# Early half products of the first up and input weight tiles, placed in the tails of the two projections before them

## The reference, cut to what matters

```python
y_l = merge_groups(conv_l, attn_l, w_o, b_o)              # cat @ w_o + b_o
x_mid = layer_norm(ALPHA * x + g1 * y_l, ln1_g, ln1_b)
h = x_mid * (1 + sc2) + sh2
u = dwconv(h @ w_up, dw_w, dw_b)                          # 1024 -> 2 * 2816
g, val = jnp.split(u, 2, axis=-1)
f_l = (silu(g) * val) @ w_down + b_down                   # 2816 -> 1024
x = layer_norm(ALPHA * x_mid + g2 * f_l, ln2_g, ln2_b)
# second block: rms_norm, scale and shift, then the second input projection
z = h2 @ w_in_2
```

## Time and profile before

| | us |
|---|---|
| median of 3 runs | 2505.81 |
| lowest and highest | 2502.83, 2510.84 |
| profiled execution, whole | 2498.72 |
| its span | 2496.8 |
| busy in the span: PE, PEld, DVE, ACT, POOL | 2275.4, 1130.6, 862.4, 485.3, 385.9 |

### The profile page before, as it was taken

How to read it: one execution, slowest core, us unless ns; L and a number is a source line. 1 busy time by engine, 2 the same in 40 slices (tenths; PEclk the granted TensorE clock), 3 DMA queues, 4 the chain that set the end, 5 groups by cost and what they waited for, 6 DMA issues and landing times. The chain is left out here.

```text
span 2496.8 us, 25488 instructions
## 1 busy us (share of the span) xinstructions
PE 2275.4 (91%) x9835; PEld 1130.6 (45%) x9835; DVE 862.4 (35%) x1468; ACT 485.3 (19%) x937; POOL 385.9 (15%) x755
## 2 busy tenths in 40 slices
PE   6998988999998998999967999888879999999985
PEld 3443654443443443444334488535434444444432
DVE  3456843222221130001888533423711111111116
ACT  2013552111110011001235422101011111111111
POOL 0004000400000000000000000000044444444424
PEclk9999999999999998998868999998989999999997
DMA  8502002455424113981202100302089999899867
GB/s 365 208 37 82 29 1 90 154 196 181 146 86 156 47 68 127 382 312 47 76 9 91 63 3 3 135 34 84 1 352 394 413 383 375 335 415 376 360 254 284
DMA packets 68553, 446.42 MB, mean 179 GB/s; under 512 B 12227, under 2 KB 12883, under 8 KB 43505
## 3 DMA queue, kind: packets, MB, share of 16 engines
q0 software_dynamic: 36176, 254.42, 25.8%
q1 hardware_dynamic: 32290, 190.78, 19.8%
HBM read 416.27 MB, written 73.45 MB: 196 GB/s over the span
## 5 line engine op out<-in xcount | busy, mean ns | idle before, releaser
L2533 PE MATMUL psum<-arena 128*64 128x512 f32 (+1 forms) x1088 | 360.6, 595 | 0.8 <-DMA arena<-in_exp_gu,arena 0.8
L938 PE MATMUL psum<-arena 128*128 128x512 f32 x704 | 307.2, 596 | 3.3 <-PEq L870 3.3
L2533 PEld LDWEIGHTS psum<-arena 128*64 128x64 f32 (+1 forms) x1088 | 138.8, 164 | 186.1 <-issue 185.1
L938 PEld LDWEIGHTS psum<-arena 128*128 128x128 f32 x704 | 133.3, 191 | 177.2 <-issue 177.2
L2524 PE MATMUL psum<-arena 128*64 128x512 f32 (+1 forms) x544 | 186.2, 598 | 1.2 <-ACT arena L2566 1.2
L1177 PE MATMUL psum<-arena 128*128 128x512 f32 x384 | 166.9, 597 | 3.6 <-ACTq L1228 3.6
L1068 PE MATMUL psum<-arena 128*128 128x512 f32 x352 | 153.5, 598 | 7.0 <-PEq L157 7.0
L997 DVE SCALAR_TENSOR_TENSOR arena<-psum,arena 128x511 f32<-128x511 f32 x88 | 66.0, 750 | 253.3 <-ACT arena L972 251.7
L2594 DVE TENSOR_TENSOR arena<-arena,psum 128x256 f32<-128x256 f32 x51 | 21.5, 421 | 342.0 <-ACT arena L2562 342.0
L833 PE MATMUL psum<-arena 128*128 128x512 f32 x256 | 113.0, 601 | 8.8 <-DMA arena<-in_w_out 8.1
L2524 PEld LDWEIGHTS psum<-arena 128*64 128x64 f32 (+1 forms) x544 | 68.5, 163 | 113.2 <-issue 111.8
(11 more groups left out here) (508 smaller groups left out, 2956.7 us busy)
## 6 DMA issues: line engine op xcount, KB each, us to landing
scratch_expert_out<-arena SPq DMA_DIRECT2D x18, 2048.0 KB, 18.6
scratch_expert_out<-arena SPq DMA_DIRECT2D x51, 512.0 KB, 9.3
arena<-in_w_ada SPq DMA_DIRECT2D x12, 2048.0 KB, 16.7
arena<-in_ada_w POOLq DMA_DIRECT2D x12, 2048.0 KB, 8.4
arena<-in_w_up SPq DMA_DIRECT2D x22, 1024.0 KB, 4.8
arena<-in_w_in SPq DMA_DIRECT2D x9, 2048.0 KB, 9.1
arena<-in_w_down SPq DMA_DIRECT2D x5, 2048.0 KB, 8.2
arena<-in_w_o SPq DMA_DIRECT2D x2, 2048.0 KB, 8.2
```

The source lines that it names most:

```text
L938: last = pe.matmul(K.bank[2 * (n % 3) + half], w[:, k, P * half:P * half + P], K.h[:, k, :], start=(k == 0), stop=(k == KD - 1))
L2533: last = pe.matmul(K.bank[2 + s][r, :], xt[:, s, P * k + r.start:P * k + r.stop], gu[:, lane, 2 * E_FF * k:2 * E_FF * (k + 1)], start=(k = ...
```

## The change

`project_tokens` gets a callable `between`, which it calls before and after the transposes of the last row tile. The output projection passes `up_ahead(n)`: wait until row tiles 0 and 1 of `K.h` are moved (16 moves) and until weight tile n of the up projection has landed, then multiply both of its blocks with tokens 0 to 255 only, into columns 0 to 255 of banks 2n and 2n+1. In the up projection, tiles 0 and 1 then multiply tokens 256 to 511 only. The down projection's TensorE program does the same with `in_ahead`: blocks 0, 1 and 2 of the first input tile ahead of the transposes of the last row tile, block 3 behind them. In the input projection the first trip of the loop is written out, and its first tile multiplies tokens 256 to 511 only. Nothing is changed on the other engines.

```diff
+EARLY = T // 2
-def project_tokens(K, pe, lhs, tiles, per, mm, after):
+def project_tokens(K, pe, lhs, tiles, per, mm, after, between=None):
...
     after(NT - 2)
+    if between:
+        between(0)
     after(NT - 1)
+    if between:
+        between(1)
...
+            def up_ahead(n):
+                pe.wait_ge(moved.sem, 2 * KD)
+                at = K.ws_taken + n
+                pe.wait_ge(K.ws_landed[at % 2].sem, 16 * (at // 2 + 1))
+                w = K.ws[:, at % 2, 0:KD * 2 * P].rearrange("p (k m) -> p k m", k=KD)
+                for half in range(2):
+                    for k in range(KD):
+                        pe.matmul(K.bank[2 * n + half][:, 0:EARLY], w[:, k, P * half:P * half + P], K.h[:, k, 0:EARLY], start=(k == 0), stop=(k == KD - 1))
...
+                    rest = slice(EARLY if n < 2 else 0, T)
                     for k in range(KD):
-                        last = pe.matmul(K.bank[2 * (n % 3) + half], w[:, k, P * half:P * half + P], K.h[:, k, :], start=(k == 0), stop=(k == KD - 1))
+                        last = pe.matmul(K.bank[2 * (n % 3) + half][:, rest], w[:, k, P * half:P * half + P], K.h[:, k, rest], start=(k == 0), stop=(k == KD - 1))
...
+            def in_ahead(blocks):
+                pe.wait_ge(moved.sem, 2 * KD)
+                at = K.ws_taken
+                pe.wait_ge(K.ws_landed[at % 2].sem, 16 * (at // 2 + 1))
+                w = K.ws[:, at % 2, :].rearrange("p (k m) -> p k m", k=KD)
+                for b in blocks:
+                    for k in range(KD):
+                        pe.matmul(K.bank[b][:, 0:EARLY], w[:, k, P * b:P * b + P], K.h[:, k, 0:EARLY], start=(k == 0), stop=(k == KD - 1))
+
+            in_ahead((0, 1, 2))
             turn_rows(K, pe, z, NT - 1, scaled, turned)
+            in_ahead((3,))
...
-            with pe.Fori(0, 3) as i:
+            for s in range(2):
+                w = take_in_loop(K, pe, 0, s).rearrange("p (k m) -> p k m", k=KD)
+                rest = slice(0 if s else EARLY, T)
+                for b in range(4):
+                    pe.wait_ge((act_out, dve_out)[b % 2].sem, 2 * s + b // 2 + 1)
+                    for k in range(KD):
+                        last = pe.matmul(K.bank[4 * s + b][:, rest], w[:, k, P * b:P * b + P], K.h[:, k, rest], start=(k == 0), stop=(k == KD - 1))
+                    last.then_inc(summed.sem, 1)
+            with pe.Fori(1, 3) as i:
```

More of the change, by code:

```diff
@@ L872, in _ @@
         def _(pe):
-            project_tokens(K, pe, K.cat, 2, 4, mm, lambda t: turn_rows(K, pe, K.res, t, normed, turned))
+            def up_ahead(n):
[6 more added lines that the diff above has]
+                        pe.matmul(K.bank[2 * n + half][:, 0:EARLY], w[:, k, P * half:P * half + P], K.h[:, k, 0:EARLY], start=(k == 0), stop=(k == KD - 1))
+            project_tokens(K, pe, K.cat, 2, 4, mm, lambda t: turn_rows(K, pe, K.res, t, normed, turned), up_ahead)
         @block.sync
```

## The result

| | before | changed |
|---|---|---|
| median of 5 runs, us | 2502.83 | 2487.70 |
| lowest and highest | 2497.92, 2510.84 | 2487.12, 2492.60 |
| profiled execution, whole | 2498.72 | 2487.70 |
| its span | 2496.8 | 2485.7 |

The ratio of the changed kernel's time to that of before is 0.9948, 95% interval 0.9932 to 0.9965: 13 us faster, between 9 and 17. The forecast was a gain of 12.4 us, a median of 2493.4 us and a profiled execution of 2486.3; the two came out at 2487.70. The median lies 5.7 us under its forecast: 3.0 of that because the median of before fell from 2505.81 over three runs to 2502.83 over five, 2.7 because the two medians now lie 15.1 us apart.

A forecast was written before the change was run, and what follows sets the result against it. TensorE, busy 91% of the span, was taken as the bound, with 21.2 us idle in two tails. Gaining 14.9 and losing 2.5 gave 12.4 us, from 2505.81 to a median of 2493.4 us, range 2485 to 2502.

The forecast's parts named there:

- The gain of the second tail: Down projection's tail and input projection: early products fill TensorE's idle gaps and keep its clock up, gaining 14.9 us.
- half records: Products of 256 columns: 218.4 ns each against 214.7 for half a full one, costing 0.5 us in each tail.
- The first tail as a loss: Output projection's tail and up projection: weights land late, early products delay the last transposes and the opening; loses 2.5 us.
- the low clock there: First 32 early up products start with the clock low: 1.65 us lost, 8.6 us in all.
- The boundary: From the last engine's end to the up projection's opening: 0.6 us.
- The third up tile: Up projection: its weight load meets POOL's 16 KB packets at a third of the rate; TensorE waits 4.7 us.
- the tile served sooner: Rival: third up tile's weights land earlier, TensorE waits 1.4 to 2.3 us; total gain 17.4 to 16.5 us; chance 0.23.
- the tile served last: Rival: third up tile's weights wait for all POOL's large packets, landing at 460.0; total gain 8.5 us; chance 0.12.
- the weight loads as the bound: Rival: weight loads pace half-width products, a half record taking as long as a full one; 35 us slower; chance 0.04.
- a gain given back later: Rival: a later stage following another clock than TensorE's returns the gain; only 0 to 5 us faster; chance 0.08.
- The sum: Whole kernel: 14.9 us gained less 2.5 lost, 12.4 us faster, forecast median 2493.4 us.
- the written-out trip: Input projection loop's first trip, peeled: changes no wait for a bank or tile, cost 0.

The follow-up runs named there:

- 15.4 alone: Changed kernel keeping only the input projection's early products, up projection as before: median 2483.69 against 2502.95 us before, ratio 0.9918.
- the halved kernel: Kernel before, with every up projection product done in two halves of 256 columns: 519.19 us from row tile 2's turn to the down projection's, 2.5 more.
- the kernel with the up part alone: Changed kernel keeping only the early products of the up projection's first two tiles; down and input projection as before: median 2500.08 us, ratio 0.9985 against before.

## Why the prediction was right, point by point

- **The gain of the second tail, 14.9 us**: 15.35 measured, 15.4 alone. The steps hold one by one: 10.36 us for 48 records (10.48), transposes 0.7 us late and at full clock, block 3 beside the moves. The 0.45 us more are half records at 216 ns instead of 218.4 (the prediction's 3.75 ns over half a full record measured 1.2), and a boundary of 0.45 us after TensorE's last drain instead of 0.66.
- **The first tail as a loss, 2.5 us**: 3.5 measured, 3.2 alone. The first up tile landed 4.7 us after its issue (4.8), the wait was 4.03 (4.1), the transposes stood behind the early products. The wrong size is the low clock there: the prediction gave the first 32 records 8.6 us, 1.65 of them for the clock, and they took 9.9, since the clock stayed low for 5.9 us of the stream and not for the 3.0 to 3.6 that the earlier trace rows show for full-width streams. The half width is not the reason, as the halved kernel's stream, after a rest of 3.24 us, had the clock back in 2.9 us; why it took longer here stays open. The boundary, 0.3 instead of 0.6, gave some of it back. The 0.6 was taken from the other tail; at this boundary the kernel before already took 0.31 us (ScalarE's moves end at 426.04, the phase opens at 426.35). The phase opened 23.2 us after the turn of tile 2, forecast 22.4.
- **The third up tile**: wait 4.69 us, forecast 4.7; landing 11.5 us, forecast 11.4; nothing moved for at least 3.4 us, forecast 3.2; share 39% over 452:456, forecast a third. The two misses are small and of opposite sign, so that the landing agrees better than its terms. The low clock behind it ran from 459.03 to 462.2, 1.6 us lost, forecast 1.65. The rule of the Trainium skill (DMA: Bandwidth & Descriptors, section on queues, rings and completion order), by which a queue is served for a group of descriptors at a time, would have had the tile land 2.4 us earlier, by the prediction's estimate. The queues' even packet counts in two kernels, 81 to 79 and 72 to 70, and above all the alternation of single packets in the changed kernel's trace are against it in this case.
- **The rivals**: the tile served sooner and the tile served last are out by its landing; the weight loads as the bound by the halved kernel; a gain given back later by stretch I, which keeps its 15.4 us in six kernels, and the stage behind it, which is no longer than before.
- **The sum**: -15.35 + 3.5 = -11.9 us in the stretches against a forecast of -12.4, and a ratio that says -13. That these agree so well is partly luck, as the ratio has an interval of 9 to 17 us and the whole may also hold the 3 us of the written-out trip, which the prediction put at nothing. The two profiled executions lie 11.0 us apart.

## What to carry to other kernels

Work moved into a tail pays when its operands are there when the tail begins; look up first when the load was issued and when it lands, since the same edit was worth 15 us where the weights had landed 10 us before and cost 3 where they came 4 us late, so that the early products stood ahead of the critical transposes and the third tile of weights was late behind them. Halving a tile's work ahead of a load also halves the cover of that load: ask which queue it now meets, and in what packet sizes. When both waits are taken away (read the slot earlier, let the other queue wait for the one tile), the same early products gain 10 us in the first tail.

## What the runs showed of the hardware

- Two DMA queues with work were served packet for packet: 81 packets of 8 KB against 79, of which 64 had 16 KB, gave 39% and 61% of the time, and 72 of 8 KB against 70 of mostly 4 KB gave 68% and 33%. The start and end times of the packets show them in turn, one by one. A tile issued while POOL's queue was at work moved nothing for over 3 us after its issue, whether that queue had packets of 16 KB (3.4 us in the changed kernel) or of 4 KB (3.3).
- After a rest of 4.03 us the low clock lasted 5.9 us into a stream of half-width products (5.6 in the kernel with the up part alone, rest 4.10), and after one of 4.69 us in the same kernel 3.1 us into a full-width stream. After a rest of 3.31 us the following 16 records took 3.23 us in one execution and 1.92 in another. What the clock cost after one rest was thus not a constant: 0 to 3 us.
- Splitting a float32 record of 512 columns in two cost 2.4 ns a pair, with twice the weight loads; a product is two such records.
- Writing out one trip of a loop of three made a kernel about 3 us quicker (interval 0.5 to 6) with both neighbouring stretches unchanged; unexplained.
